# Two-block transformer on one core: the second block's latent attention in two query tiles, with projections placed between its steps

## The reference

```python
# second block, layer 1
kv_a = rmsnorm(h, norm_kv_g) @ w_kv_a                    # 512 latent + 64 rotary
c_kv = rmsnorm(kv_a[:, :512], kv_a_norm_g)
k_rope = apply_rope(kv_a[:, 512:])
k_nope, v = per head: c_kv @ w_kv_b                      # 8 heads x (128 + 128)
cq = rmsnorm(rmsnorm(h) @ w_q_a, q_a_norm_g)             # rank 768
q = per head: cq @ w_q_b                                 # 8 heads x (128 + 64 rotary)
scores = q @ k.T * 192**-0.5, masked to keys of the same or an earlier 64-token chunk
h = h + concat_heads(softmax(scores) @ v) @ w_o          # w_o: 1024 x 1024
h = h + (silu(hn @ w1) * (hn @ w3)) @ w2                 # 1024 -> 2816 -> 1024
return rmsnorm(h, final_g)[:, 16:]                       # the 16 meta tokens are dropped
```

## Time and profile before

| | us |
|---|---|
| median of 3 runs | 1866.47 (1854.03 to 1883.77) |
| the profiled execution | 1867.1 |
| its span, first to last instruction | 1865.3 |
| PE busy | 1630.9 (87%) |
| PEld, DVE, ACT, POOL busy | 1333.9, 749.0, 590.1, 179.5 |
| mean granted TensorE clock | 0.904 of full speed |

### The profile page before, as it was taken

The page is one execution under the profiler, slowest core; times in us unless marked ns, Lnnn a source line. Parts: engine busy times, 40 slices in busy tenths (PEclk is TensorE's granted clock), DMA queues, the critical chain, the costliest instruction groups (busy, mean ns, idle before and its releaser), DMA issues.

```text
span 1865.3 us, 28689 instructions
## 1 busy us (share of the span) xinstructions
PE 1630.9 (87%) x12348; PEld 1333.9 (72%) x12348; DVE 749.0 (40%) x1232; ACT 590.1 (32%) x888; POOL 179.5 (10%) x119
## 2 busy tenths in 40 slices
PE   6999798897777767775899998899997999989997
PEld 5998556865444444443888868899997865689997
DVE  5355844341111111122743543555445453355543
ACT  4347543211111101012333322334334442243432
POOL 2000000100000000000100011144203100024410
PEclk8999898978978888787999998999998976999999
DMA  6421100089999999996343321344353340034341
GB/s 268 164 108 75 71 20 1 15 365 426 428 429 428 428 429 429 428 428 282 113 168 132 117 95 46 126 176 155 138 193 124 113 189 1 1 127 170 138 154 44
DMA packets 31991, 361.09 MB, mean 194 GB/s; under 512 B 5281, under 2 KB 8225, under 8 KB 9633
## 3 DMA queue, kind: packets, MB, share of 16 engines
q1 hardware_dynamic: 31904, 359.84, 48.0%
HBM read 358.78 MB, written 1.05 MB: 193 GB/s over the span
## 4 chain that ended last, share of the span: by engine, by line
PE 67%; DMA 18%; DVE 7%; ACT 4%; issue 2%; SPq 1%; POOL 1%; DVEq 0%; ACTq 0%; PEld 0%; PEldq 0%
PE PS L448 38%; DMA expert_w<-in_w 17%; PE PS L461 5%; PE PS L647 3%; PE PS L806 3%; PE PS L490 3%; PE PS L673 3%; PE PS L471 2%; PE PS L922 2%; PE PS L826 2%; ACT wh L1070 2%; PE PS L657 2%; DVE wl L1456 2%; DVE rs L1471 1%; SPq L323 1%
## 5 line engine op out<-in xcount | busy, mean ns | idle before, releaser
L1456 DVE TENSOR_TENSOR wl<-raw,wh 128x4096 fp32r<-128x4096 f32 (+2 forms) x77 | 315.8, 4101 | 317.0 <-ACT wh L1070 317.0
L448 PE MATMUL PS<-UH,wh 128*128 128x272 f32 x1160 | 338.3, 292 | 17.3 <-DVE wl L1496 9.6
L448 PE MATMUL PS<-UH,wl 128*128 128x272 f32 x1160 | 335.7, 289 | 0.0
L448 PE MATMUL PS<-UL,wh 128*128 128x272 f32 x1160 | 334.6, 288 | 0.0
L1070 ACT ACTIVATE wh<-raw 128x4096 fp32r<-128x4096 f32 (+2 forms) x78 | 261.9, 3358 | 186.1 <-PE PS L448 169.6
L806 PE MATMUL PS<-expert_w,XW 128*32 128x256 f32 x2048 | 168.5, 487 | 92.0 <-DMA expert_w<-in_w 91.9
L448 PEld LDWEIGHTS PS<-UH,wh 128*128 128x128 f32 x1160 | 219.5, 189 | 19.6 <-DVE wl L1496 10.0
L448 PEld LDWEIGHTS PS<-UL,wh 128*128 128x128 f32 x1160 | 220.1, 190 | 0.5
L448 PEld LDWEIGHTS PS<-UH,wl 128*128 128x128 f32 x1160 | 219.4, 189 | 0.0
L806 PEld LDWEIGHTS PS<-expert_w,XW 128*32 128x32 f32 x2048 | 76.5, 134 | 172.6 <-issue 85.8
L1788 DVE TENSOR_TENSOR SG<-PS,SG 128x128 f32<-128x128 f32 x32 | 9.3, 292 | 302.0 <-ACT SG L1261 302.0
(11 more groups left out here) (385 smaller groups left out, 2788.3 us busy)
## 6 DMA issues: line engine op xcount, KB each, us to landing
expert_w<-in_w SPq DMA_DIRECT2D x96, 2048.0 KB, 21.4
raw<-in_up SPq DMA_DIRECT2D x22, 2048.0 KB, 8.4
raw<-in_down SPq DMA_DIRECT2D x16, 1408.0 KB, 5.9
raw<-in_ret_qk SPq DMA_DIRECT2D x4, 2048.0 KB, 10.6
raw<-in_ret_v SPq DMA_DIRECT2D x4, 2048.0 KB, 8.5
raw<-in_ret_gate SPq DMA_DIRECT2D x4, 2048.0 KB, 8.4
raw<-in_ret_o SPq DMA_DIRECT2D x4, 2048.0 KB, 9.1
raw<-in_q_b SPq DMA_DIRECT2D x3, 1536.0 KB, 6.5
```

Of the source, the lines that this page charges most:

```text
L448: mm = pe.matmul(gbank(g)[:, 0:T], w[:, c:c + P], x(k), start=(k == 0 and j == 0), stop=(k == nk - 1 and j == 2))
L1456: dve.tensor_tensor(WL[n % 2][:, 0:w], RAW[n % 3][:, 0:w], WH[n % 2][:, 0:w].bitcast(F32), ALU.subtract).then_inc(lo_done, 1)
```

## The change

1. The latent attention gets a loop of its own of 16 steps: two query tiles of 128 for each head, meta queries left out. Tile 0 reads 144 keys, tile 1 all 272 (the chunk mask excludes the rest). `weighted` becomes four matmuls: 256 columns over keys 0 to 127, then 16, 112 and 32 keys, each for the query tile that needs them (128 columns).
2. The slabs are cut anew: `kv_a` and `kv_b` hold keys and values of four heads each, `q_r` the rotary queries, `q_a` and `q_b` the others of four heads each. Before the attention run `kn0` to `kn3`, the values of heads 0 to 3 (3 units), `qr`, `qn0`, `qn1`. The other 13 units (`qn2` to `qn7`, `kn4` to `kn7`, `vb0` to `vb2`) are put between the scores and the transposes of steps 0 to 11. Slabs `kv_b`, `q_b` and the first of `mla_o` are split in quarters, which ACT and DVE take between their steps.
3. Everything of the last layer that isn't keys or values works on columns 16 to 271: `qar`, three of four `krq` units, `qn`, `qr`, `mo`, `up1`, `down1`, their norms and the final norm.
4. Transposes of at least 128 source columns, in the sparse attention of the first block, in `utok`, ahead of the stick-breaking part and in the latent attention, are issued in TensorE's transpose mode.
5. `mo` waits head by head for `OMH`/`OML` and not for all. SP loads the mask (now 2 tiles, at another address) earlier, ahead of slab `q_b`. The scalars of the softmax get a tile of their own.

```diff
+MLA_STEPS = [(h, t) for h in range(HEADS) for t in range(2)]
+MLA_KEYS = [144, T]
+MLA_FILL = {0: ("qn2",), 1: ("qn3",), 2: ("kn4", "kn5"), 3: ("kn6",), 4: ("kn7",), 5: ("qn4",), 6: ("vb0",),
+            7: ("qn5",), 8: ("vb1",), 9: ("vb2",), 10: ("qn6",), 11: ("qn7",)}
+MLA_PIECES = {0: (("kv_b", 2),), 1: (("kv_b", 3),), 2: (("q_b", 0),), 3: (("q_b", 1),),
+              4: (("q_b", 2), ("q_b", 3)), 10: (("mla_o", 0),), 11: (("mla_o", 1),), 12: (("mla_o", 2),),
+              13: (("mla_o", 3),)}
 # SP
-            for n in range(FIRST_SLAB["kv_c"], FIRST_SLAB["mla_o"] + 4):
+            for n in range(FIRST_SLAB["kv_c"], FIRST_SLAB["kv_b"] + 1):
                 slab(n)
-            sp.wait_ge(unit_done, UNIT0["om0"])
+            sp.wait_ge(nrm_done, 24 + 8 * 5 + 2)
             load(NEG2[:], a["neg"], mla_in)
 # PE
-                        mm = pe.matmul(gbank(g)[:, 0:T], w[:, c:c + P], x(k),
+                        mm = pe.matmul(gbank(g)[:, c0:T], w[:, c:c + P], x(k)[:, c0:],
+            def turn(dst, src, m, n, first):
+                if n < P:
+                    return pe.matmul(dst, src, ident[0:m, 0:m], start=first, stop=True, skip_group_check=True)
+                return pe.matmul(dst, src, ident[0:m, 0:m], start=first, stop=True, is_transpose=True,
+                                 skip_group_check=True)
...
+            late("qn0")
+            rotate_mla(1)
+            rotate_mla(2)
+            late("qn1")
+            rotate_mla(3)
             rotate_mla(4)
             pe.wait_ge(rot_done, 15)
...
+                pe.matmul(sbank(i % 2)[:, 0:nk], QN[:, h, q0:q0 + P], KN[:, h, 0:nk], start=True, stop=False)
+                pe.matmul(sbank(i % 2)[:, 0:nk], QR[r, h // 2, q0:q0 + P], KR2[r, 0:nk], start=False, stop=True)
...
+                turn(b[:, 0:P], PR2[i % 2][:, 0:P], P, P, True)
+                if t == 0:
+                    turn(b[0:16, P:2 * P], PR2[i % 2][:, P:P + 16], P, 16, False).then_inc(at_t, 1)
+                else:
+                    turn(b[:, P:2 * P], PR2[i % 2][:, P:2 * P], P, P, False)
+                    turn(b[0:32, 2 * P:3 * P], PR2[i % 2][:, 240:272], P, 32, False).then_inc(at_t, 1)
...
+            mla_scores(0)
+            for i, (h, t) in enumerate(MLA_STEPS):
+                if i + 1 < len(MLA_STEPS):
+                    mla_scores(i + 1)
+                if t == 0 and h:
+                    mla_weighted(h - 1)
+                for name in MLA_FILL.get(i, ()):
+                    late(name)
+                mla_turned(i)
+            mla_weighted(HEADS - 1)
 # ACT, per step: exponential of i+1, copies of i, read-outs of the units, quarters of a slab
+                for name in MLA_FILL.get(i, ()):
+                    late_out(name)
+                for name, q in MLA_PIECES.get(i, ()):
+                    hi_part(FIRST_SLAB[name], q)
+            hi(FIRST_SLAB["mla_o"] + 1)
 # DVE, per step: scaling of i, maxima of i+1, at t == 1 the split of head h-1, quarters
+                if i + 1 < len(MLA_STEPS):
+                    mla_maxima(i + 1)
+                if t == 1 and h:
+                    split_out(UNIT0[f"om{h - 1}"], slice(0, P), OMH[:, h - 1, META:], OML[:, h - 1, META:], SEQ)
+                for name, q in MLA_PIECES.get(i, ()):
+                    lo_part(FIRST_SLAB[name], q)
+            split_out(UNIT0["om7"], slice(0, P), OMH[:, 7, META:], OML[:, 7, META:], SEQ)
+            lo(n + 1)
 # DVE, ahead of the attention
+            lo(FIRST_SLAB["q_a"])
+            lo_part(FIRST_SLAB["kv_b"], 0)
+            for j in range(2):
+                rotated(11 + j, QR[:, j, META:], ROT_M, META)
+            lo_part(FIRST_SLAB["kv_b"], 1)
+            for j in range(2, 4):
+                rotated(11 + j, QR[:, j, META:], ROT_M, META)
```

More of the change, by code:

```diff
@@ L995, in _ @@
             for u in range(1, 4):
-                product(UNIT0["krq"] + u, n + 1, 8 * u, KB, *U2)
+                product(UNIT0["krq"] + u, n + 1, 8 * u, KB, *U2, c0=META)
             norm_sum(SQQ, 4)
@@ L1021, in rotate_mla @@
                     pe.wait_ge(rot_free, 10 + j - 3)
-                pe.matmul(sbank(j % 4)[:, 0:T], rot[:], t, start=True, stop=True).then_inc(rot_mm, 1)
+                pe.matmul(sbank(j % 4)[:, c0:T], rot[:], t, start=True, stop=True).then_inc(rot_mm, 1)
+            pe.wait_ge(nlo_done, 8 * 5 + 10)
+            pe.wait_ge(nhi_done, 8 * 5 + 10)
             rotate_mla(0)
-            for s in range(3):
-                slab_ready(n + s)
-                for u in range(4):
-                    product(UNIT0["qn"] + 4 * s + u, n + s, 6 * u, 6,
-                            lambda k: CQH[:, k, :], lambda k: CQL[:, k, :])
-                    if s == 2 and u:
-                        rotate_mla(u)
+            slab_ready(FIRST_SLAB["q_r"])
@@ new lines, in _, with late @@
+            for u in range(4):
+                product(UNIT0["qr"] + u, FIRST_SLAB["q_r"], 6 * u, 6, *CQ, c0=META)
+            def late(name):
+                g, h = UNIT0[name], int(name[2:])
+                if name[:2] == "qn":
+                    n = FIRST_SLAB["q_a" if h < 4 else "q_b"]
+                    if h % 4 == 0:
+                        slab_ready(n)
+                    product(g, n, 6 * (h % 4), 6, *CQ, c0=META)
+                elif name[:2] == "kn":
+                    n = FIRST_SLAB["kv_b"]
+                    if h == 4:
+                        slab_ready(n)
+                    product(g, n, 4 * (h - 4), 4, *CK)
+                else:
+                    token_major(g, FIRST_SLAB["kv_b"], 4, 512, 16 * P, *CKT, TOK3[h])
@@ L1379, in ffn @@
                         hi(n + s + 2)
-                    square_of_sum(sq_next, f"down{layer}", s)
+                    square_of_sum(sq_next, f"down{layer}", s, c0)
             ffn(0, 32, SQM)
@@ L1426, in _, with values @@
-            hi(FIRST_SLAB["kv_c"] + 6)
-            for s in range(3):
-                for u in range(4):
-                    j = 4 * s + u
-                    read_out(UNIT0["qn"] + j, QN[:, j, :] if j < 8 else QR[:, j - 8, :])
-                hi(FIRST_SLAB["q_b"] + s + 2)
-            attention(PR2, PT2, (P + HD) ** -0.5, "om", lambda h: None)
+            def values(g, j, c):
+                if j < 2:
+                    read_out(g, VM[:, j, c], cols=slice(0, 512))
+                else:
+                    read_out(g, VM[0:32, j, c], rows=slice(96, P), cols=slice(0, 512))
@@ new lines, in late_out @@
+            def late_out(name):
+                g, h = UNIT0[name], int(name[2:])
+                if name[:2] == "qn":
+                    read_out(g, QN[:, h, late], cols=late)
+                elif name[:2] == "kn":
+                    read_out(g, KN[:, h, :])
+                else:
+                    values(g, h, slice(512, 1024))
+            for j in range(3):
+                values(UNIT0["va_m"] + j, j, slice(0, 512))
+            hi(FIRST_SLAB["q_a"])
+            for u in range(4):
+                read_out(UNIT0["qr"] + u, QR[:, u, late], cols=late)
```

340 lines of the change are left out of this document (210 added, 130 removed).

## The result

The changed kernel took 1799.93 us, the median of four runs (1798.15 to 1812.47), against 1873.21 for the kernel before in the same session (four runs, 1854.03 to 1883.77): ratio 0.9675, 95% interval 0.9616 to 0.9735. Forecast were 1813 us. The profiled execution took 1799.95 us, its span 1798.0. Medians are printed over all executions, but ratios, intervals and ranges called compared leave out those over 1.5% above their kernel's fastest (here 1883.77 of before), so a ratio isn't the quotient of the two medians printed.

A forecast was written before the change was run, and what follows sets the result against it. The prediction took TensorE's busy time and its granted clock to bound the kernel outside the transfer-bound experts. Its terms, 0.3 + 5.3 + 28.7 + 7 + 0 + 11.2 + 0.7 = 53.2, off 1867.1 gave 1813 us, own range 1793 to 1830.

The forecast's parts named there:

- sparse attention and transposes ahead: First block: 48 transposes in transpose mode save 0.11 us each, 5.3 us; three ahead of the stick-breaking part save 0.3.
- attention starts earlier: Last layer, ahead of the latent attention: units moved into the loop and trimmed columns, less 1.1 us waiting, give 28.7 us.
- attention: Latent attention: 70.8 us of PE work, 10 of waits and 5 of clock make 86 against 93.0, 7 us gained.
- output projection: After the latent attention: 192 matmuls lose 1.4 us, DVE's low part adds 1.5; nothing in total.
- feed-forward, norms: Last feed-forward: 1056 + 528 matmuls save 7.1 ns each, 11.2 us; norm sums, scaling and last stores save 0.7.
- the other low stretches of the span: Low-clock stretches elsewhere in the kernel, said to shift with every start and spread the runs; no size given.
- The rival by which the mode doesn't do what it says: All transposes in transpose mode: still two records, or one as long; 8 us back, 1821 us; chance 0.10.
- Pitches: fp32r matmuls: 16 columns fewer save 7.1 ns, so a 256-column one takes 0.1186 us instead of 0.126.
- the chain through a quarter: Latent attention loop: transposes, copies, read-out, ACT's and DVE's quarter, then scaling for the next transposes take 4.1 us.
- the low stretch at the loop's start: Start of the latent attention: some 10 us at the low clock after PE idles 3 us, half of it lost, 5.
- The first rival: Sparse and latent attention both run mostly at the low clock: 52 and 43 us more, 1908 us; chance 0.05.
- 48 x 0.16: Sparse attention: saving of its 48 transposes if transpose mode were four times faster for float32, 7.9 us and not 5.3.

The follow-up runs named there:

- b0: The kernel before, unchanged, profiled a second time: 1854.45 us.
- e1: The changed kernel with every transpose an ordinary float32 matmul again: 1817.8 us, ratio 0.9753.
- e8: The changed kernel with ordinary transposes in the new latent attention alone, units left between its steps: 1804.87 us, ratio 0.9679.
- e2: The changed kernel with the last feed-forward and its norms on all 272 columns again: 1811.28 us, ratio 0.9708.
- e7: The changed kernel with all 13 units ahead of the latent attention and ordinary transposes in its bare loop: 1789.3 us, ratio 0.9619.
- e9: e3 unchanged, run once more in other executions: 1813.68 us, ratio 0.9725.
- b2: The kernel before with transpose mode in the first block only, ordinary transposes in its old latent attention: 1870.21 us, ratio 1.0007.
- e3: The changed kernel with all 13 units ahead of the latent attention, its bare loop keeping transpose mode: 1812.14 us, ratio 0.9706.
- e5: The changed kernel with slab quarters spread over more steps and 36 output-projection matmuls moved into steps 13 to 15: 1802.37 us, ratio 0.9633.

## Why the prediction was right, point by point

The time lay 13 us under the forecast (14 under its sum, 1813.9) and inside its range. The terms, measured as b0 less after, where the rest of the kernel ran alike:

| term | predicted, us | measured, us |
|---|---|---|
| sparse attention and transposes ahead | 5.6 | 6.2 |
| attention starts earlier | 28.7 | 28.9 |
| attention | 7 | 6.8 |
| output projection | 0 | 2.1 |
| feed-forward, norms | 11.9 | 10.7 |
| sum | 53.2 | 54.7 |

*What made the 13 us.* The sum was near (53.2 against 54.7), and made against one execution, which had 8.1 us of low clock in the retention layer that neither b0 nor after has. The prediction named "the other low stretches of the span" in its own range (1793 to 1830) but gave no sign to them, so that the time lay below 1813 and not above it is the luck of these executions. How much the change gains on average is less sure than the table looks: b0 (1854.45) is near the fastest of before, whose sessions have medians from 1865 to 1875, and the ratio's interval is 50 to 72 us. That the typical gain is 55 and not 65 isn't shown.

*Transposes.* Rows of the sparse attention in after, PE in order of time:

```profile
232.59 0.44 PE L485 MATMUL PS<-ident,PR 128*128 128x128 f32 x2
232.96 0.41 PE L484 MATMUL PS<-ident,PR 128*32 128x128 f32 x2
233.29 0.72 PE L667 MATMUL PS<-KR,QB 64*128 64x272 f32 x2
```

A 128-row tile takes 233.29 - 232.59 = 0.70 where it took 0.98. Its two full transposes (L485) are two records, one for each call, and the one of 32 columns, still ordinary (L484), is two. The expected single record for a transpose is there. The 16 transposes of `utok` show it too, before and after:

```profile
375.39 5.18 PE L736 MATMUL PS<-ident,UM 128*128 128x128 f32 x32
```

```profile
369.43 3.65 PE L485 MATMUL PS<-ident,UM 128*128 128x128 f32 x16
```

In the tile a full transpose takes 0.37/2 = 0.185 us against (0.98 - 0.33)/2 = 0.325, so it saves 0.14 where the sum had 0.11: the prediction took 0.21 to 0.22 for an ordinary one, from the row of `utok`, and between scores it costs more. Seven heads by busy time:

```profile
231.17:286.19 55.02, 55.02 (x227) 24.99 (x226) 28.28 (x120) 24.69 (x94) 0.00 (x0) 1.00 0.08 34
```

That is 7.86 us a head, forecast 7.9, before 8.53. The rival by which the mode doesn't do what it says falls (one record, and a shorter one; e1).

*Pitches.* Forecast 0.1186 by the line through the earlier trace rows; in the feed-forward 22 pitches of 256 columns lie between these two rows, (1652.42 - 1649.81)/22 = 0.1186:

```profile
1649.81 0.28 PE L462 MATMUL PS<-UH,wl 128*128 128x256 f32 x1
...
1652.42 0.28 PE L462 MATMUL PS<-UH,wh 128*128 128x256 f32 x1
```

*The start of the attention.* 28.9 against 28.7. PE waited for the last rotation, 3.0 by the forecast:

```profile
1470.65 0.51 PE L1079 MATMUL PS<-KN,QN 128*128 128x144 f32 x2 [2.38 <-DVE QR L1661]
```

*The attention.* The total was right with two errors that cancel. Idle time was 86.21 - 78.39 = 7.8 us against 10: the chain through a quarter was sized well (transposes at 1539.59, the next at 1543.77: 4.2 against 4.1), and it showed in step 13 (2.40) and step 5 (2.50), but steps 3, 11 and 12 hid it better than thought (0.77 and 0.40). The clock cost more than the 5 us given, and elsewhere; this part of the mechanism was wrong. I put the low stretch at the loop's start, by the idle time ahead of it, and had the units hold the level up behind it. At the start it lasted 3.4 us; the long one, 20.5, came at the end, in the steps with no unit, for which the sum had nothing. About half of PE's busy time in these stretches is loss: 3.4/2 and (16.2 - 3.1)/2 inside the loop, some 8 us. What is left, 78.4 - 8.2 = 70.2, is PE's work at the high level, forecast 70.8.

*Output projection.* Costed at nothing, for +1.5 of DVE's low part against -1.4 of columns. PE's busy time fell by 2.27 (31.43 to 29.16), 1.4 of it the columns and the rest clock (0.92 against 0.90), and its idle time rose by 0.2 only: the low part in front of the first sum into H was hidden nearly whole.

*The first rival* didn't come in the changed kernel's four executions, but the sparse attention did run low in others. In the profiled executions of e8 (1860.26 us) and e2 (1857.79) it had the low level nearly to its end; e8's row:

```profile
229.20:333.50 104.30, 103.04 (x249) 43.46 (x249) 32.47 (x134) 27.08 (x103) 0.00 (x0) 0.53 0.05 23
```

These executions were 55 and 47 us above their kernels' medians (8 of the 55 are e8's retention layer); the prediction had 52 for this attention low alone, 1865 in all. Of 60 executions with transpose mode in the first block six lie 35 us or more above their kernel's median, of 53 without it one. That would fit a cost of the mode there too, but only two of the seven have a trace, so it isn't shown.

*The page's rule.* Transpose mode and the clock: the pair e7 and e9 shows 1.00 against 0.53 in one loop by the mode alone. The Trainium skill (TensorE: Matmul & The Clock Gate, "Part 4: PE-mode transpose") says that the mode doesn't count as PE being busy in the same way. The pair agrees. e1 and e8 show that the changed kernel's loop doesn't pay for the mode, and the old loop shows 54.6 to 99.0 us low without any mode (before, b0, b2), which that rule doesn't explain. The prediction gave the low clock a small chance partly because the loop would get dense units; e3 shows that with the mode this was the reason that counted. The Trainium skill has a factor of four for float32 in the same page's list of terms. The traces don't agree: 0.325 against 0.185 us for a full transpose is a factor of 1.8. By four, the prediction's 48 x 0.16 is 7.7 us (it says 7.9) in the sparse attention; measured were 6.2, transposes ahead of it included.

*What stays open.* Why the loop of before fell low for 54.6 or 99.0 us with ordinary transposes and e7's never did. They differ in the idle time ahead (1.96 us, and next to none), in the wait ahead of the first transposes (2.19 us against 0.83), in the 16-row tiles, and in the first step's wait for a whole slab; none of these was tried alone. And why e1 and e8, with ordinary transposes and units in steps 0 to 11, fell low for 24 and 20.5 us at the loop's end, in float32 steps like those that e7 ran at the high level without any unit.

*The best version* is e7, 1789.3 us: ratio to before 0.9619 against 0.9675, its four runs all under the changed kernel's four, though the intervals overlap and the two weren't run in one session. It keeps the two tiles, the trimmed columns and the mode in the first block, and gives up the units between the steps.

## What to carry to other kernels

Look at the granted clock of a loop before its busy share: a PE that was 97% busy ran the same steps in 74 or in 48 us. An instruction that saves time by itself (transpose mode, 0.28 us a tile) can cost many times that through the clock in a loop of float32 steps alone; price it in both surroundings, and price each part of a change without the others: here the units between the steps paid only together with the mode. When work is moved forward to fill a gap, follow what it waits for and what it then waits behind: e5 gained no clock from its units and took two new waits, for a quarter not yet split and behind a low part that now stood in front. And a prediction made against one profile inherits its luck; take a second profile of the kernel before, if it can be had.

## What the hardware showed

- A float32 transpose of 128 columns is one record in transpose mode and two otherwise; between scores, at the high level, it takes 0.185 us instead of 0.325, a tile of 272 keys 0.70 instead of 0.98.
- One loop, same instructions, PE about 95% busy: clock 0.70, 0.70, 0.56 in three profiles (before, b0, b2).
- Transpose mode alone, in a loop of float32 scores and transposes: 0.53 against 1.00 (e3 and e9, e7), 26 us in one loop.
- A low stretch of 17 us can come in the retention layer's float32 products, behind an idle time of 2.04 us, in one execution and not in the next (before and b0; e8 has it again).
- The executions of one kernel on one core spread by more than 30 us (before, 1852.74 to 1891.3 in 17 runs), and the granted clock goes with it: 0.916 in the execution of 1852.74 us, 0.891 in that of 1891.3.
